# Score products of running streams on quarters of the TensorE columns, with the output projection and two norms laid between them

## The chip, the cores and the metric

The kernel runs on one core of one Trainium2 chip. The metric is the device time of one execution in microseconds (us). Five engines matter: TensorE (PE, with its weight load PEld), VectorE (DVE), ScalarE (ACT), GpSimd (POOL) and SyncE (SP), which here issues nearly all loads. Everything is in fp32: a matmul stands in the trace as two records, a transposition as one.

## The reference

One layer of a streaming encoder for 512 prompt rows and 8 running streams of 16 rows each (128 sample rows), so 640 rows of 1024 channels in 5 tiles of 128. The part around the change:

```python
q, k, v = parallel_mixer_inputs(...)           # 8 heads of 64, q and k normed
s = einsum('bqhd,bkhd->bhqk', q, concat(cache_k, k)) * 64**-0.5 + bias   # samples: 512 cached keys + 16 new
o = einsum('bhqk,bkhd->bqhd', softmax(s), concat(cache_v, v))
cat = concatenate([rms_norm(y_ssm, g1), rms_norm(y_att, g2)])            # 512 + 512 channels
x = x + cat @ w_out                                                      # 1024 x 1024
mk = rms_norm(mem_k, gain)                                               # memory keys, 256 tokens, 4 heads of 256
x = x + memory_attend(rms_norm(x), mk, mv)                               # cross-attention
x = x + hier_moe(rms_norm(x))
```

## The kernel before

The program is written out by hand for each engine. The function `pe_order` lists every product of TensorE up to the experts in the order in which it is made. Product number n goes to PSUM bank n mod 8; `claim(pe, key)` makes TensorE wait until the product eight places earlier in the list has been drained, and `done(eng, key)` makes another engine wait until a product is ready. So the list sets the order of the work and also who waits for whose bank. VectorE, ScalarE and GpSimd each run their own hand-written sequence, strictly in order.

The stages around the change are these.

- **Prompt attention.** 32 units (4 row tiles t by 8 heads). TensorE makes the scores of unit i (L926, key `S`), turns the probabilities of unit i-2 (L943, `PT`), and after every second unit makes their product with the values (L961, `PV`). VectorE adds the bias (L1873), takes the maximum (L1876, L1880) and the reciprocal of the sum (L1888); ScalarE does the exponential (L1313) and drains the turned tiles (L1330); GpSimd multiplies by the reciprocal (L1531). VectorE copies `PV` out (L1911).
- **Sample attention.** Eight steps, one for each stream b. `qblk` holds for each stream and each of the 4 head pairs a block 128 columns wide, zero outside the pair's own 32 columns; four matmuls add up into a 128 x 512 score tile `sA` (L971, the cached keys) and four into a 128 x 128 tile `sB` (L975, the new keys). The rest of the step works on earlier streams: turn the probabilities of b-1 (`sPa`, `sPb`, L943), multiply those of b-2 with the values (`sPV`, L989, 32 columns for each pair), transpose the result of b-3 (`sO`, L995), which VectorE copies out in `spv_out` (L1918). SP loads 1 MB of keys and 1 MB of values for each stream into two buffers each: keys b are issued once `sB` of b-2 is made, and values b once `sPV` of b-2 is made (L702, L707).
- Between the steps VectorE also does the **branch norms**: the squares of both 4 x 640 branch outputs, their sums over the 4 channel tiles (L1951), and the multiplication by the gains (L1956).
- **Output projection.** Ten pairs of products `oS` (state-space branch) and `oA` (attention branch), 4 matmuls of 128 x 512 each (L775). After the first four stands `ss` (L1020), ten matmuls of one column that finish the sums of squares. VectorE waits for GpSimd's inverse root (L1481) and adds every product to the residual rows (L2026, L2029). From the second row tile on, the finished rows are turned (`x1T`, L1001) and drained (L2000). Ahead of the third row tile VectorE norms the memory keys: squares and sums (L1599, L2008), then two multiplications for each of four parts (L1599, L2017). Then TensorE turns them (`mkT`, L1032).
- **The next stage** begins with the query projection `mq` of the cross-attention; its weights are loads 11 and 12 (L625). Load 11 waits for `ss`, load 12 for `oA` 8. After `mk_normed` GpSimd stores the memory keys and issues fourteen stores of zeros (L1537 to L1542).

The experts' stage at the end streams 96 MB of weights through five buffers.

```python
for a in range(NPAIR):   # sA of stream b, before
    last = nc.tensor.matmul(ps, qblk[:, b, a, :], kc[b % 2][:, a, :], start=(a == 0), stop=(a == 3))
```

Of the kernel before, what the change touches and what calls it, by code (L numbers as in the profile page):

```python
# [22 lines left out]
P = 128  # L23
D = 1024
# [54 lines left out]

def pe_order():  # L80
# [73 lines left out]
    for t in range(NT + 1):  # L154
# [6 lines left out]
        if t >= 1:  # L161
# [15 lines left out]
           11: ("ss", 0), 12: ("oA", 8), 13: ("oA", 9), 14: ("mq", 8)}  # L177
# [18 lines left out]
def program(nc, x_t, x_rows, mem_t, mem_rows, dense_w, exp_gu, exp_dn, ck_t, cv, cmk_t, cmv, cols, k_gain, mk_gain,  # L196
# [3 lines left out]
    with ctx:  # L200
# [131 lines left out]
        qblk = at(R + 10240, NB, NPAIR, P)  # L332
# [288 lines left out]
        def _(sp):  # L621
# [98 lines left out]
            sp.dma_start(mk_rows, mk_dram.ap().rearrange("(t p) d -> p t d", p=P)).then_inc(S["mem_landed"], 16)  # L720
# [50 lines left out]
        def _(pe):  # L771
# [193 lines left out]
            pe.wait_ge(S["qblk_ready"], 1)  # L965
            for b in range(NB + 3):
                if b < NB:
                    ps = claim(pe, ("sA", b))
                    pe.wait_ge(S[f"kc{b % 2}"], 16 * (b // 2 + 1))
                    for a in range(NPAIR):  # L970
                        last = nc.tensor.matmul(ps, qblk[:, b, a, :], kc[b % 2][:, a, :], start=(a == 0), stop=(a == 3))  # L971
                    last.then_inc(product_ready, 1)
                    ps = claim(pe, ("sB", b))
                    for a in range(NPAIR):
                        last = nc.tensor.matmul(ps[:, 0:P], qblk[:, b, a, :], kT[:, a, TP:T], start=(a == 0), stop=(a == 3))  # L975
                    last.then_inc(product_ready, 1)
# [28 lines left out]
            wo = [w_at(9), w_at(10)]  # L1005
            for t in range(NT + 1):
                if t < NT:

                    pe.wait_ge(S["branch_scaled"], 2 if t < NT - 1 else 3)
                    for c in range(2):  # L1010
                        for kind, k0, src in (("oS", 0, ysT), ("oA", 4, yaT)):
                            dense((kind, 2 * t + c), lambda k: src[:, k, tok(t)],
                                  lambda k: wo[c][:, k0 + k, :], 512, 4)
                if t == 0:

                    ps = claim(pe, ("ss", 0))
                    pe.wait_ge(S["sq_ready"], 3)
                    for br in range(2):
                        for j in range(NT):
                            last = nc.tensor.matmul(ps[:, br * NT + j:br * NT + j + 1], branch_sum[br][:, tok(j)], ones[:, 0:1],  # L1020
                                                    start=True, stop=True)
                    last.then_inc(product_ready, 1)
                if t >= 1:
                    for hh in range(2):
                        pe.wait_ge(drained["oA"], 2 * t - 1 + hh)
                        turn_rows("x1T", 2 * t - 2 + hh)
# [135 lines left out]
        def _(act):  # L1162
# [179 lines left out]
            for i in range(n + 2):  # L1342
                if 2 <= i < n:
                    exp_prompt(i)
                if i >= 2:
                    pt_out("PT", i - 2, i - 2, PROMPT_UNITS[i - 2][0] + 1)
            for b in range(NB + 2):
                if b < NB:
# [119 lines left out]
        def _(pool):  # L1468
# [120 lines left out]
        def _(dve):  # L1589
# [331 lines left out]
            attn_in(0)  # L1921
# [477 lines left out]
```

## Time and profile before

| | |
|---|---|
| three runs, median (lowest to highest) | 1109.52 us (1106.23 to 1111.93) |
| the profiled execution, its own time | 1107.45 us |
| its span, first to last instruction | 1105.7 us |
| PE, DVE, ACT, POOL busy | 88%, 38%, 18%, 15% |
| chain that ended last | PE 68%, DMA 16%, DVE 7% |
| mean granted clock of TensorE | 0.913 of full speed |

Times in the rows are microseconds from the start of the span. TensorE's granted clock is given as a share of 2.4 GHz, so 0.50 is 1.2 GHz. Busy shares are averages over stages; which wait ends last has to be read stage by stage.

### The profile page before, as it was taken

What the parts mean: (1) busy time and instruction counts of PE and PEld (TensorE: products, weight loads), DVE (VectorE), ACT (ScalarE), POOL (GpSimd) and SP (SyncE); (2) the same over time, 40 slices, a digit from 0 to 9 for tenths busy, and PEclk for the clock granted to TensorE, in tenths of its full rate; (3) what the DMA queues carried; (4) which work ended last, traced back from release to release, by engine and by line L of the source; (5) the groups of instructions that cost most, each with busy time, mean ns of one, the idle gap of its engine ahead of it and who ended that gap; (6) DMA issues with size and microseconds to landing.
All of it is one profiled execution on the core that took longest, in us unless ns stands there. A gap on an engine that the chain in (4) does not pass through costs nothing.

```text
span 1105.7 us, 12501 instructions
## 1 busy us (share of the span) xinstructions
PE 969.3 (88%) x4646; PEld 546.7 (49%) x4646; DVE 422.7 (38%) x1061; ACT 201.0 (18%) x450; POOL 165.7 (15%) x202
## 2 busy tenths in 40 slices
PE   6999988997989988899999898999389998797780
PEld 2444454544454455554544674455356565464350
DVE  1723638554254456335433531233633111110114
ACT  2311140214033312100100232011001111111110
POOL 0223100000034322204011330000101000000003
PEclk9999988998965589999999899999589999988895
DMA  9641324255330026725700436820559999999937
GB/s 358 258 55 60 79 91 157 95 175 202 153 152 1 1 77 232 301 78 205 289 0 18 174 143 238 371 85 20 220 207 425 426 425 425 424 425 427 427 162 285
DMA packets 45515, 230.67 MB, mean 209 GB/s; under 512 B 5632, under 2 KB 12296, under 8 KB 32960
## 3 DMA queue, kind: packets, MB, share of 16 engines
q1 hardware_dynamic: 33008, 185.94, 42.9%
q0 software_dynamic: 9712, 33.98, 9.1%
q10 hardware_dynamic: 2736, 9.96, 2.2%
q8 instruction: 38, 0.62, 0.2%
q14 instruction: 21, 0.17, 0.0%
HBM read 196.41 MB, written 31.35 MB: 206 GB/s over the span
## 4 chain that ended last, share of the span: by engine, by line
PE 68%; DMA 16%; DVE 7%; issue 3%; SPq 2%; POOL 2%; ACT 1%; POOLq 0%; DVEq 0%; ACTq 0%
PE banks L775 33%; DMA arena<-in_exp_gu 12%; PE banks L519 8%; PE banks L926 3%; PE banks L805 3%; PE banks L531 2%; PE banks L943 2%; DVE arena L1599 2%; SPq L676 2%; PE banks L961 2%; PE banks L971 1%; DMA arena<-in_ck_t 1%; PE banks L1081 1%; PE banks L1110 1%; DMA arena<-in_x_t 1%
## 5 line engine op out<-in xcount | busy, mean ns | idle before, releaser
L775 PE MATMUL banks<-arena 128*128 128x512 f32 (+1 forms) x976 | 416.8, 581 | 5.1 <-DVE arena L2043 3.0
L775 PEld LDWEIGHTS banks<-arena 128*128 128x128 f32 x976 | 182.4, 191 | 208.2 <-issue 203.5
L519 PE MATMUL banks<-arena 128*64 128x256 f32 (+1 forms) x1024 | 143.9, 400 | 25.0 <-DMA arena<-in_exp_gu 22.2
L519 PEld LDWEIGHTS banks<-arena 128*64 128x64 f32 (+1 forms) x1024 | 102.8, 155 | 72.7 <-issue 42.7
L1599 DVE TENSOR_TENSOR arena<-arena 128x16 f32<-128x16 f32 (+13 forms) x224 | 91.7, 410 | 87.7 <-ACT arena L1373 35.2
L531 PE MATMUL banks<-arena 128*64 128x512 f32 (+1 forms) x256 | 69.7, 600 | 9.0 <-ACT arena L1445 9.0
L2293 DVE SCALAR_TENSOR_TENSOR arena<-arena,banks 128x256 f32<-128x256 f32 x19 | 8.0, 421 | 162.4 <-ACT arena L1440 162.4
L1531 POOL TENSOR_SCALAR arena<-arena 128x128 f32<-128x128 f32 (+4 forms) x40 | 49.7, 1243 | 133.0 <-DVE arena L1888 133.0
L1567 POOL DMA_INDIRECT arena<-xn_scratch,tok_idx x19 | 18.6, 978 | 230.5 <-PE banks L513 209.6
L1480 POOL TENSOR_SCALAR arena<-arena 128x2 f32<-128x2 f32 (+4 forms) x30 | 6.3, 210 | 285.7 <-DVE arena L1792 114.7
L805 PE MATMUL banks<-arena 128*128 128x512 f32 x80 | 37.8, 635 | 9.5 <-DMA arena<-in_dense_w 8.5
L531 PEld LDWEIGHTS banks<-arena 128*64 128x64 f32 (+1 forms) x256 | 22.4, 146 | 44.4 <-issue 30.9
L1313 ACT ACTIVATE arena<-banks,arena 128x128 f32<-128x128 f32 (+3 forms) x48 | 25.1, 525 | 102.4 <-DVE arena L1880 96.5
L1876 DVE TENSOR_REDUCE arena<-banks 128x1 f32<-128x256 f32 (+3 forms) x68 | 32.0, 471 | 26.0 <-PE banks L1094 17.5
L943 PE MATMUL banks<-arena 128*128 128x128 f32 x120 | 30.1, 376 | 13.4 <-POOL arena L1531 13.3
L926 PE MATMUL banks<-arena 64*128 64x128 f32 (+3 forms) x64 | 41.8, 757 | 0.0
L943 PEld LDWEIGHTS banks<-arena 128*128 128x128 f32 x120 | 17.3, 181 | 40.1 <-issue 24.7
L1481 POOL TENSOR_TENSOR arena<-arena 128x2 f32<-128x2 f32 (+4 forms) x30 | 33.9, 1130 | 2.5
L1450 ACT ACTIVATE arena<-banks 128x512 f32<-128x512 f32 x38 | 22.7, 597 | 60.2 <-PE banks L531 60.2
L971 PE MATMUL banks<-arena 128*128 128x512 f32 x64 | 31.5, 636 | 1.8 <-DMA arena<-in_ck_t 1.8
L805 PEld LDWEIGHTS banks<-arena 128*128 128x128 f32 x80 | 16.1, 204 | 30.4 <-issue 28.6
L1873 DVE TENSOR_TENSOR banks<-banks,arena 128x128 f32<-128x128 f32 (+1 forms) x48 | 17.4, 362 | 29.9 <-PE banks L926 16.8
(277 smaller groups left out, 961.5 us busy)
## 6 DMA issues: line engine op xcount, KB each, us to landing
arena<-in_exp_gu SPq DMA_DIRECT2D x32, 2048.0 KB, 26.8
arena<-in_exp_dn SPq DMA_DIRECT2D x32, 1024.0 KB, 29.5
arena<-in_dense_w SPq DMA_DIRECT2D x14, 2048.0 KB, 9.8
moe_scratch<-arena ACTq DMA_DIRECT2D x19, 512.0 KB, 9.8
arena<-in_ck_t SPq DMA_DIRECT2D x8, 1024.0 KB, 7.2
arena<-in_cv SPq DMA_DIRECT2D x8, 1024.0 KB, 5.6
arena<-in_cmk_t SPq DMA_DIRECT2D x8, 1024.0 KB, 6.8
arena<-in_cmv SPq DMA_DIRECT2D x8, 1024.0 KB, 5.4
```

Source lines behind the costliest of these rows:

```text
L519: last = nc.tensor.matmul(banks[r0:r0 + n, 2 + half, 0:FF], x[:, k, r0:r0 + n], w[:, k, half * FF:(half + 1) * FF], start=(k == 0), stop=( ...
L531: last = nc.tensor.matmul(banks[r0:r0 + n, 6 + c, :], ht[:, f, r0:r0 + n], w[:, f, c * 512:(c + 1) * 512], start=(f == 0), stop=(f == 1))
L775: last = nc.tensor.matmul(ps[:, 0:n], lhs(i), rhs(i), start=(i == 0), stop=(i == k - 1))
L805: last = nc.tensor.matmul(ps, hT[:, k, tok(t)], w[:, k, :], start=(k == 0), stop=(k == KT - 1))
L926: nc.tensor.matmul(ps[:, 0:P * (t + 1)], qT[lo:lo + HD, h // 2, tok(t)], kT[lo:lo + HD, h // 2, 0:P * (t + 1)], start=True, stop=True).the ...
L943: last = nc.tensor.transpose(ps[:, a, :], Pb[unit % 3][:, (first + a) * P:(first + a + 1) * P], ident)
L971: last = nc.tensor.matmul(ps, qblk[:, b, a, :], kc[b % 2][:, a, :], start=(a == 0), stop=(a == 3))
L1313: ins = A(Pb[i % 3][:, c0:c0 + n], bank(key)[:, 0:n], ACT.Exp, bias=smax[:, i % 4, 2:3], accum_out=ssum[:, i % 4, j:j + 1])
L1481: g.tensor_tensor(dst, mean, minus_half[:, 0:n], ALU.pow).then_inc(signal, 1)
L1531: g.tensor_scalar(Pb[i % 3][:, 0:w], Pb[i % 3][:, 0:w], ssum[:, i % 4, 3:4], None, ALU.mult).then_inc(S["p_scaled"], 1)
L1599: link(v.tensor_tensor(o, a, b, op))
L1876: link(v.tensor_reduce(smax[:, i % 4, j:j + 1], ps[:, 0:n], AXX, ALU.max))
```

## The change

The score products of a sample write each head pair's 32 rows of the tile with a matmul of their own that uses a 32-column block of `qblk` (now 32 wide) and neither starts nor ends a sum with the others. The scores of stream 0 are made at the end of the prompt units. The output projection's products 0 to 7 of both branches, which read prompt rows alone, are listed in the sample steps (`OUT_FILL`): one `oS` and one `oA` in steps 1 to 8, `oS` 8 and 9 in steps 9 and 10. `ss` is split in two: nine columns ahead of step 1, one after the samples. The branch norms of the state-space half go to prompt units 4, 6 and 8, those of the attention half to units 12 to 14, 20 to 22, 28 to 30 and behind the last unit, and for the sample rows to the end. The sums for the memory keys are taken in VectorE's step 4, the multiplications in its steps 6 and 7, and their load moves up behind keys 2. Load 11 waits for the second `ss`.

```diff
 
+OUT_FILL = [[]] + [[("oS", i), ("oA", i)] for i in range(8)] + [[("oS", 8)], [("oS", 9)]]
...
     for i in range(10):
@@ -106,25 +109,24 @@
             o.append(("S", i))
         if 0 <= i - 2 < n:
             o.append(("PT", i - 2))
+        if i == n:
+            o += [("sA", 0), ("sB", 0)]
         if i >= 4 and (i - 4) % 2 == 1 and i - 4 < n:
             o.append(("PV", (i - 4) // 2))
+    o.append(("ss", 0))
     for b in range(NB + 3):
-        if b < NB:
+        if 0 < b < NB:
             o += [("sA", b), ("sB", b)]
+        o += OUT_FILL[b]
         if 0 <= b - 1 < NB:
             o += [("sPa", b - 1), ("sPb", b - 1)]
         if 0 <= b - 2 < NB:
             o.append(("sPV", b - 2))
         if 0 <= b - 3 < NB:
             o.append(("sO", b - 3))
-    for t in range(NT + 1):
-        if t < NT:
-            for c in range(2):
-                o += [("oS", 2 * t + c), ("oA", 2 * t + c)]
-        if t == 0:
-            o.append(("ss", 0))
-        if t >= 1:
-            o += [("x1T", 2 * t - 2), ("x1T", 2 * t - 1)]
+    o += [("x1T", i) for i in range(4)]
+    o += [("ss", 1), ("oA", 8), ("oA", 9)]
...
 W_AFTER = {3: ("u", 4), 5: None, 6: ("v", 4), 7: ("mk", 1), 8: ("mk", 3), 4: ("mv", 1), 9: ("mv", 3), 10: ("mv", 3),
-           11: ("ss", 0), 12: ("oA", 8), 13: ("oA", 9), 14: ("mq", 8)}
...
-        qblk = at(R + 10240, NB, NPAIR, P)
+        qblk = at(R + 10240, NB, NPAIR, 32)
+        key_sq = at(R + 11264, D)
...
             load_keys(2)
+            done(sp, ("PT", len(PROMPT_UNITS) - 1))
+            sp.dma_start(mk_rows, mk_dram.ap().rearrange("(t p) d -> p t d", p=P)).then_inc(S["mem_landed"], 16)
             for b in range(3, NB):
                 load_keys(b)
                 load_values(b - 1)
             load_values(NB - 1)
 
             done(sp, ("sB", NB - 1))
-            sp.dma_start(mk_rows, mk_dram.ap().rearrange("(t p) d -> p t d", p=P)).then_inc(S["mem_landed"], 16)
+            sp.wait_ge(S["mk_stats"], 1)
...
+            def sample_scores(b):
+
+                ps = claim(pe, ("sA", b))
+                pe.wait_ge(S[f"kc{b % 2}"], 16 * (b // 2 + 1))
+                for a in range(NPAIR):
+                    last = nc.tensor.matmul(ps[32 * a:32 * a + 32, :], qblk[:, b, a, :], kc[b % 2][:, a, :], start=True, stop=True)
+                last.then_inc(product_ready, 1)
+                ps = claim(pe, ("sB", b))
+                for a in range(NPAIR):
+                    last = nc.tensor.matmul(ps[32 * a:32 * a + 32, 0:P], qblk[:, b, a, :], kT[:, a, TP:T], start=True, stop=True)
+                last.then_inc(product_ready, 1)
+
+            def out_products(products):
+                for kind, i in products:
+                    wo = w_at(9 + i % 2, i < 2)
+                    k0, src, scaled = (0, ysT, 1) if kind == "oS" else (4, yaT, 5 if i < 8 else 6)
+                    pe.wait_ge(S["branch_scaled"], scaled)
+                    dense((kind, i), lambda k: src[:, k, tok(i // 2)], lambda k: wo[:, k0 + k, :], 512, 4)
+
+            def square_sums(i, columns):
+                ps = claim(pe, ("ss", i))
+                for br, j in columns:
+                    last = nc.tensor.matmul(ps[:, br * NT + j:br * NT + j + 1], branch_sum[br][:, tok(j)], ones[:, 0:1],
+                                            start=True, stop=True)
+                last.then_inc(product_ready, 1)
...
+                if i == n:
+                    pe.wait_ge(S["qblk_ready"], 1)
+                    sample_scores(0)
...
-            pe.wait_ge(S["qblk_ready"], 1)
+            pe.wait_ge(S["sq_ready"], 1 + NT - 1)
+            square_sums(0, [(0, j) for j in range(NT)] + [(1, j) for j in range(NT - 1)])
             for b in range(NB + 3):
-                if b < NB:
-                    ps = claim(pe, ("sA", b))
-                    pe.wait_ge(S[f"kc{b % 2}"], 16 * (b // 2 + 1))
...
+                if 0 < b < NB:
+                    sample_scores(b)
+                out_products(OUT_FILL[b])
                 if 0 <= b - 1 < NB:
...
-            wo = [w_at(9), w_at(10)]
-            for t in range(NT + 1):
-                if t < NT:
-
-                    pe.wait_ge(S["branch_scaled"], 2 if t < NT - 1 else 3)
-                    for c in range(2):
-                        for kind, k0, src in (("oS", 0, ysT), ("oA", 4, yaT)):
...
+            def x1_turn(i):
+                pe.wait_ge(drained["oA"], i + 1)
+                turn_rows("x1T", i)
+
+            for i in range(4):
+                x1_turn(i)
+            pe.wait_ge(S["sq_ready"], 1 + NT)
+            square_sums(1, [(1, NT - 1)])
+            out_products([("oA", 8), ("oA", 9)])
+            for i in range(4, 10):
+                x1_turn(i)
...
+                if i == n:
+                    exp_unit(n, [(("sA", 0), 512, 0), (("sB", 0), P, 512)])
...
-            pool.wait_ge(drained["ss"], 1)
-            rsqrt_mean(rstd_g, ssg, 2 * NT, AW, S["rstd_g_ready"])
-            pool.wait_ge(S["mk_stats"], 1)
-            rsqrt_mean(qf8, qss8, 8, MD, S["mk_factor"])
+                if i == n:
+                    pool.wait_ge(drained["ss"], 1)
+                    rsqrt_mean(rstd_g[:, 0:2 * NT - 1], ssg[:, 0:2 * NT - 1], 2 * NT - 1, AW, S["rstd_g_ready"])
+                if i == n + 4:
+                    pool.wait_ge(S["mk_stats"], 1)
+                    rsqrt_mean(qf8, qss8, 8, MD, S["mk_factor"], col=32)
+            pool.wait_ge(drained["ss"], 2)
+            rsqrt_mean(rstd_g[:, 2 * NT - 1:2 * NT], ssg[:, 2 * NT - 1:2 * NT], 1, AW, S["rstd_g_ready"], col=20)
             pool.wait_ge(S["mk_normed"], 4)
...
-                    c0 = (2 * a + h2) * SQ
-                    ins = v.tensor_copy(qblk[lo:lo + HD, :, a, c0:c0 + SQ],
+                    ins = v.tensor_copy(qblk[lo:lo + HD, :, a, SQ * h2:SQ * h2 + SQ],
...
+            def branch_step(i):
+
+                if i == 4:
+                    dve.wait_ge(drained["gv"], 4)
+                    dve.wait_ge(drained["gs"], 4)
+                    branch_squares(ysT, slice(0, T), 0)
+                if i == 6:
+                    branch_sums(0, slice(0, T))
+                if i == 8:
+                    branch_scale(ysT, out_ssm, slice(0, T))
+                t, step = (i - 12) // 8, (i - 12) % 8
+                cols = slice(t * P, (t + 1) * P)
+                if i >= 12 and step == 0:
+                    dve.wait_ge(drained["PV"], 4 * t + 4)
+                    branch_squares(yaT, cols, 1)
+                if i >= 12 and step == 1:
+                    branch_sums(1, cols)
+                if i >= 12 and step == 2:
+                    branch_scale(yaT, out_att, cols)
...
+                branch_step(i)
             attn_out(n - 1)
+            attn_in(n)
             pv_out(n // 2 - 2)
             pv_out(n // 2 - 1)
...
+            for i in (n + 4, n + 5, n + 6):
+                branch_step(i)
+
+            def out_rows(kind, i):
+                x = xr[:, i // 2, (i % 2) * 512:(i % 2 + 1) * 512]
+                col = i // 2 + (0 if kind == "oS" else NT)
+                done(dve, (kind, i))
+                if kind == "oA":
+                    dve.wait_ge(drained["oS"], i + 1)
+                v.scalar_tensor_tensor(x, bank((kind, i)), rstd_g[:, col:col + 1], x, ALU.mult, ALU.add).then_inc(drained[kind], 1)
...
+            def mem_key_sums():
+                dve.wait_ge(S["mem_landed"], 32)
+                for t in range(2):
+                    tt(key_sq, mk_rows[:, t, :], mk_rows[:, t, :], ALU.mult)
+                    ins = v.tensor_reduce(qss8[:, 4 * t:4 * t + 4], key_sq.rearrange("p (h d) -> p h d", h=MH), AXX, ALU.add)
+                    if t == 0:
+                        link(ins)
+                ins.then_inc(S["mk_stats"], 1)
+
+            def mem_key_rows(i):
+                seg = mk_rows[:, i // 2, (i % 2) * 512:(i % 2 + 1) * 512].rearrange("p (h d) -> p h d", h=2)
+                f = qf8[:, 4 * (i // 2) + 2 * (i % 2):4 * (i // 2) + 2 * (i % 2) + 2]
+                tt(seg, seg, spread(f.unsqueeze(2), [P, 2, MD]), ALU.mult)
+                v.tensor_tensor(seg, seg, spread(mkg.unsqueeze(1), [P, 2, MD]), ALU.mult).then_inc(S["mk_normed"], 1)
...
-            def norm_mem_keys():
-
-                dve.wait_ge(S["mem_landed"], 48)
...
-            for t in range(NT):
-                if t == 2:
-                    norm_mem_keys()
...
+            dve.wait_ge(S["x_landed"], 32)
+            for b in range(1, NB + 1):
+                attn_out(n + b - 1)
+                if b == 1:
+                    done(dve, ("ss", 0))
+                    ps = bank(("ss", 0))
+                    link(v.tensor_scalar(ssg[:, 0:NT], ps[:, 0:NT], 1.0 / 16, None, ALU.mult))
+                    v.tensor_copy(ssg[:, NT:2 * NT - 1], ps[:, NT:2 * NT - 1]).then_inc(drained["ss"], 1)
+                if b >= 2:
+                    dve.wait_ge(S["rstd_g_ready"], 1)
+                    out_rows("oS", b - 2)
+                    out_rows("oA", b - 2)
+                if b < NB:
+                    attn_in(n + b)
+                if b >= 3:
+                    spv_out(b - 3)
+                if b == 4:
+                    mem_key_sums()
+                if b >= 6 and b < 8:
+                    dve.wait_ge(S["mk_factor"], 1)
+                    mem_key_rows(2 * (b - 6))
+                    mem_key_rows(2 * (b - 6) + 1)
+            out_rows("oS", 7)
+            out_rows("oA", 7)
+            spv_out(NB - 2)
+            out_rows("oS", 8)
+            spv_out(NB - 1)
+
+            dve.wait_ge(drained["sO"], NB)
+            branch_squares(yaT, slice(TP, T), 1)
+            branch_sums(1, slice(TP, T))
+            branch_scale(yaT, out_att, slice(TP, T))
+            out_rows("oS", 9)
+            for i in range(4):
+                turn_out("x1T", i, norm_mem)
+            done(dve, ("ss", 1))
+            v.tensor_copy(ssg[:, 2 * NT - 1:2 * NT], bank(("ss", 1))[:, 2 * NT - 1:2 * NT]).then_inc(drained["ss"], 1)
+            dve.wait_ge(S["rstd_g_ready"], 2)
+            out_rows("oA", 8)
+            out_rows("oA", 9)
+            for i in range(4, 10):
+                turn_out("x1T", i, norm_mem)
```

## Rows read from the trace of the kernel before

**Rows 1.** Busy time of each engine by stage, with granted clock, DMA share and GB/s

```profile
318.00:338.00 20.00, 19.86 (x62) 9.31 (x63) 10.73 (x42) 7.12 (x27) 8.58 (x10) 0.50 0.25 95
395.00:464.00 69.00, 58.99 (x501) 36.79 (x498) 39.23 (x87) 16.13 (x56) 15.06 (x8) 0.91 0.59 211
464.00:541.00 77.00, 77.00 (x237) 38.55 (x236) 33.57 (x48) 7.09 (x13) 16.74 (x22) 1.00 0.55 204
```

**Rows 2.** Chain that ended last, samples to next stage: start, us, what

```profile
395.24 4.45 PE banks L971 x8
...
440.81 7.42 DMA arena<-in_ck_t
448.37 3.67 PE banks L971 x8
452.04 0.89 PE banks L975 x8
452.93 0.55 PE banks L943 x5
453.48 1.23 PE banks L989 x40
...
463.74 13.91 PE banks L775 x32
477.64 2.13 PE banks L1020 x20
...
537.44 1.75 PE banks L1001 x16
...
540.93 20.68 PE banks L775 x48
...
668.91 3.58 PE banks L1110 x16
```

**Rows 3.** VectorE's branch norms among the samples, by shape

```profile
L1951 DVE TENSOR_REDUCE arena<-arena 128x640 f32<-128x2560 f32 x1 | 4.6, 4564 | 0.0
...
L1599 DVE TENSOR_TENSOR arena<-arena 128x2560 f32<-128x2560 f32 x1 | 2.8, 2826 | 0.0
```

**Rows 4.** Timeline of the first prompt units, all engines

```profile
313.80 0.28 DVE L1873 TENSOR_TENSOR banks<-banks,arena 128x128 f32<-128x128 f32 x1
...
314.76 0.60 POOL L1531 TENSOR_SCALAR arena<-arena 128x128 f32<-128x128 f32 x1 [0.18 <-DVE arena L1888]
...
316.31 0.47 PE L943 MATMUL banks<-arena 128*128 128x128 f32 x1
...
324.03 0.69 PE L943 MATMUL banks<-arena 128*128 128x128 f32 x2
```

**Rows 5.** Timeline around the end of a sample step

```profile
437.23 0.80 PE L943 MATMUL banks<-arena 128*128 128x128 f32 x5 [2.12 <-POOL arena L1531]
...
437.96 2.36 PE L989 MATMUL banks<-arena 128*32 128x128 f32 x40
...
447.84 0.33 PE L995 MATMUL banks<-arena 128*128 128x128 f32 x1
...
448.21 0.46 DVE L1918 COPY arena<-banks 64x64 f32<-64x64 f32 x2 [1.64 <-PE banks L995]
...
448.89 0.16 DVE L1888 RECIPROCAL arena<-arena 128x1 f32<-128x1 f32 x1
```

**Rows 6.** VectorE's drain of one output product, by shape

```profile
L2026 DVE SCALAR_TENSOR_TENSOR arena<-banks,arena 128x512 f32<-128x512 f32 x10 | 7.5, 748 | 13.0 <-PE banks L775 10.6 <-POOL arena L1481 2.4
```

**Rows 7.** Timeline of VectorE at the memory keys

```profile
495.58 1.22 DVE L1599 TENSOR_TENSOR arena<-arena 128x1024 f32<-128x1024 f32 x1
...
499.35 1.22 DVE L2008 TENSOR_REDUCE arena<-arena 128x4 f32<-128x1024 f32 x1
502.61 0.69 DVE L1599 TENSOR_TENSOR arena<-arena 128x512 f32<-128x512 f32 x1 [2.04 <-POOL arena L1481]
```

**Rows 8.** Loads issued from 520 to 536 us: size, median us to landing

```profile
arena<-in_dense_w SPq DMA_DIRECT2D x1, 2048.0 KB, 9.5
```

More of the change, by code:

```diff
@@ L119, in pe_order @@
             o.append(("sO", b - 3))
-    for t in range(NT + 1):
-        if t < NT:
-            for c in range(2):
-                o += [("oS", 2 * t + c), ("oA", 2 * t + c)]
-        if t == 0:
-            o.append(("ss", 0))
-        if t >= 1:
-            o += [("x1T", 2 * t - 2), ("x1T", 2 * t - 1)]
+    o += [("x1T", i) for i in range(4)]
+    o += [("ss", 1), ("oA", 8), ("oA", 9)]
+    o += [("x1T", i) for i in range(4, 10)]
     o += [("mkT", i) for i in range(4)]
@@ L1002, in turn_rows @@
                 last.then_inc(product_ready, 1)
-            wo = [w_at(9), w_at(10)]
-            for t in range(NT + 1):
-                if t < NT:
-                    pe.wait_ge(S["branch_scaled"], 2 if t < NT - 1 else 3)
-                    for c in range(2):
-                        for kind, k0, src in (("oS", 0, ysT), ("oA", 4, yaT)):
[L1012 to L1026, printed above, removed]
+            def x1_turn(i):
[8 more added lines that the diff above has]
+                x1_turn(i)
             for i in range(4):
@@ L1347, in _ @@
             for b in range(NB + 2):
-                if b < NB:
+                if 0 < b < NB:
                     exp_unit(n + b, [(("sA", b), 512, 0), (("sB", b), P, 512)])
@@ L1919, in spv_out, with branch_squares, branch_sums, branch_scale @@
                 ins.then_inc(drained["sO"], 1)
+            link(v.tensor_scalar(out_ssm, out_ssm, 0.25, None, ALU.mult))
+            def branch_squares(y, cols, n_sums):
+                if n_sums:
+                    dve.wait_ge(S["sq_ready"], n_sums)
+                tt(branch_sq[:, :, cols], y[:, :, cols], y[:, :, cols], ALU.mult)
+            def branch_sums(br, cols):
+                v.tensor_reduce(branch_sum[br][:, cols], branch_sq[:, :, cols].rearrange("p k t -> p t k"), AXX, ALU.add
+                                ).then_inc(S["sq_ready"], 1)
+            def branch_scale(y, gain, cols):
+                w = cols.stop - cols.start
+                v.tensor_tensor(y[:, :, cols], y[:, :, cols], spread(gain.unsqueeze(2), [P, 4, w]), ALU.mult
+                                ).then_inc(S["branch_scaled"], 1)
+            def branch_step(i):
[16 more added lines that the diff above has]
+                    branch_scale(yaT, out_att, cols)
             attn_in(0)
@@ L1954, in branch_scale @@
-            def branch_scale(y, gain, cols):
-                w = cols.stop - cols.start
-                v.tensor_tensor(y[:, :, cols], y[:, :, cols], spread(gain.unsqueeze(2), [P, 4, w]), ALU.mult
-                                ).then_inc(S["branch_scaled"], 1)
-            for b in range(NB):
-                if b >= 1:
-                    attn_out(n + b - 1)
-                attn_in(n + b)
-                if b >= 3:
-                    spv_out(b - 3)
-                if b == 0:
-                    dve.wait_ge(drained["gv"], 4)
-                    dve.wait_ge(drained["gs"], 4)
-                    branch_squares(ysT, slice(0, T), 0)
-                if b == 1:
-                    branch_sums(0, slice(0, T))
-                if b == 2:
-                    branch_scale(ysT, out_ssm, slice(0, T))
-                if b == 3:
-                    dve.wait_ge(drained["PV"], len(PROMPT_UNITS) // 2)
-                    branch_squares(yaT, slice(0, TP), 1)
-                if b == 4:
-                    branch_sums(1, slice(0, TP))
-                if b == 5:
-                    branch_scale(yaT, out_att, slice(0, TP))
@@ L1981, in _ @@
-            attn_out(n + NB - 1)
-            for b in range(NB - 3, NB):
-                spv_out(b)
-            dve.wait_ge(drained["sO"], NB)
-            branch_squares(yaT, slice(TP, T), 2)
-            branch_sums(1, slice(TP, T))
-            branch_scale(yaT, out_att, slice(TP, T))
-            done(dve, ("ss", 0))
-            ps = bank(("ss", 0))
-            link(v.tensor_scalar(ssg[:, 0:NT], ps[:, 0:NT], 1.0 / 16, None, ALU.mult))
-            v.tensor_copy(ssg[:, NT:2 * NT], ps[:, NT:2 * NT]).then_inc(drained["ss"], 1)
@@ L2019, in _ @@
-            for t in range(NT):
-                if t == 2:
-                    norm_mem_keys()
-                for c in range(2):
-                    i = 2 * t + c
-                    x = xr[:, t, c * 512:(c + 1) * 512]
-                    done(dve, ("oS", i))
-                    v.scalar_tensor_tensor(x, bank(("oS", i)), rstd_g[:, t:t + 1], x, ALU.mult, ALU.add).then_inc(drained["oS"], 1)
-                    dve.wait_ge(drained["oS"], i + 1)
-                    done(dve, ("oA", i))
-                    v.scalar_tensor_tensor(x, bank(("oA", i)), rstd_g[:, NT + t:NT + t + 1], x, ALU.mult, ALU.add).then_inc(drained["oA"], 1)
-                if t >= 1:
-                    turn_out("x1T", 2 * t - 2, norm_mem)
-                    turn_out("x1T", 2 * t - 1, norm_mem)
@@ L2033, in _ @@
-            turn_out("x1T", 8, norm_mem)
-            turn_out("x1T", 9, norm_mem)
+            dve.wait_ge(S["x_landed"], 32)
[20 more added lines that the diff above has]
+                    mem_key_rows(2 * (b - 6) + 1)
```

30 lines of the change are left out of this document (1 added, 29 removed).

## The prediction

> **What bounds the kernel now.** I read the busy time by stage first. From 464 to 541 us, the output projection, TensorE is busy all of the time at full clock: only removed or overlapped work helps there. From 395 to 464, the samples, it is busy 59.0 of 69 us. In the early prompt units (318 to 338) it is busy all the time at a granted clock of 0.50, the 1.2 GHz level; VectorE is busy for 10.7 of those 20 us [rows 1]. Then the chain of waits. A sample step is 3.67 us of `sA`, 0.89 of `sB`, 0.55 of turns, 1.23 of `sPV`, and the chain also goes through a load of keys of 7.42 us; the chain leaves the samples at 463.74 and reaches `mq` at 540.93 with TensorE's work alone [rows 2]. So all that counts is when `mq` starts. What follows should move with it as a block, since its loads and table work hang on products of its own stage.
>
> **The scores.** `sA` is 4 matmuls of 512 columns, 3.67 us for 8 records; `sB` 0.89 [rows 2]. In quarters of 32 rows, the nearest rows are `sPV`, 40 records on four column quarters in 1.23 us, 31 ns each, and the half-array products of L1110, 16 records of 512 columns in 3.58 us, 224 ns each [rows 2]. One such record alone takes 13.91/32 = 435 ns [rows 2], so halves overlap twofold. I take 8 x 112 = 0.90 us for `sA` and 8 x 31 = 0.25 for `sB`: 1.15 instead of 4.56. The bounds: all serial, 4.56, and the ideal quarter, 4.56/4 = 1.14.
>
> **The steps.** An `oS`, `oA` pair costs 13.91/2 = 6.95 us [rows 2]. A full step is 1.15 + 6.95 + 0.55 + 1.23 + 0.3 (`sO`, [rows 5]) = 10.2 us; step 1 has no `sPV` and `sO` (8.7), step 2 no `sO` (9.9), steps 3 to 7 are full (51.0), step 8 has no scores (9.0), steps 9 and 10 have half a pair (5.0 and 3.8). Sum 87.4 us. The keys are now covered: keys b+1 are issued right behind values b-1, at the end of step b-1, so they have one step, 10.2 us, against the 7.42 of the row. The load of the memory keys, moved ahead of keys 3, adds 1 MB where steps 1 and 2 give it 18 us: nothing.
>
> **What is late instead: VectorE.** In each step VectorE ends with `spv_out`, which waits for `sO`, TensorE's last product of the step. Only then come the reciprocal for b and the drain of `oS` b-1. But `oS` b takes the very bank of `oS` b-1 from step 4 on (eight products a step, eight banks). The rows give, from the start of `sO` at 447.84, the reciprocal's end at 449.05 [rows 5]; 0.75 for the drain [rows 6] makes 1.96 us. TensorE wants the bank after 0.27 + 1.15, at 1.45. So steps 4 and 6 stall 0.5 us each. Behind `spv_out` of step 4 stand the sums for the memory keys, 495.58 to 500.57 = 4.99 us [rows 7]: step 5 stalls 5.5 us. Behind that of step 6 stand four multiplications of 0.69 [rows 7], 2.7 us: step 7 stalls 3.2. Step 8 has no scores, its banks are another eight, and it stalls nothing. Together 9.7 us. The cover for GpSimd's scaling and the exponential is the pair of products between them, 6.95 us: 1.9 and 1.4 us fit.
>
> **A rule weighed.** The rows show full 128-row products drained by one 0.75 us instruction each, and VectorE at 39 of 69 us [rows 1, 6]. By the Trainium skill, page TensorEngine Tiling (Array Packing), section PSUM Bottleneck, tiling speeds the matmuls but not the drain, and the drain may become the bound. By that rule the sum is the one above; without it these 9.7 us would be left out.
>
> **The clock.** After 2.12 us without work TensorE came back at half speed: five turns took 0.80 us and `sPV` 2.36, against 0.55 and 1.23 [rows 5, 2], about 1.7 us lost until it was back. I charge that three times: at the start of step 1, and after the stalls in steps 5 and 7. 5.1 us.
>
> **Prompt units.** Squares (2.83), sums (4.56) and gains (as long as the squares) of the 2560-wide branch enter units 4, 6, 8 [rows 3]: 10.2 us on VectorE. Unit 5's maximum, begun at 313.80 before, is held until 316.7; the probabilities of unit 4 then need 1.7 us (as from 313.80 to 314.76 + 0.60 and a hop), so their turn comes at 318.5 rather than 316.31 [rows 4]. Following the same order on through the sums and the gains, unit 8's turn comes at 330.4 instead of 324.03 [rows 4]: 6.4 us. The 512-wide pieces later cost 0.6 to 1.0 each and sit in the wait for an exponential, 0.3 us in all. Total 6.7; bounds 0 (all covered) and 10.2 (none).
>
> **The joint.** The last values' product ends at 395.24 + 6.7. `sA` and `sB` of stream 0 lie where TensorE waited for GpSimd; at half clock they last 2.3 us against a wait of 1.6: +0.7. Then TensorE waits for VectorE's copy, squares and sums of the last tile, 0.3 + 0.7 + 1.0 + hops = 2.2, and nine of `ss` take 2.0 [rows 2]. Step 1 starts at 406.8.
>
> **The tail.** 406.8 + 87.4 + 9.7 + 5.1 = 509.0 for the end of the last `sO`. Squares and sums of the sample rows are ready 2.4 us later; four `x1T` (0.44 each, 1.75 for four [rows 2]) hide most of that. The gain's multiplication lets `oA` 8 start at +3.1; `oA` 8 and 9 take 6.95, six `x1T` 2.6, `mkT` 1.75; the last drain on VectorE adds 0.3: 14.7. `mq` would start at 523.7. Load 11 is issued at about +3 and has 11.7 us; the row of a load in company of the zero stores says 9.5 [rows 8], but two 1 MB loads are just ahead and GpSimd's stores start at +8.5: I add 1 us, bounds 0 and 5. GpSimd's fourteen issues end about when the first `mq` is made, so its inverse root is in time. `mq` at 524.7 instead of 540.93: 16.2 us gained. The shorter clearing of `qblk` saves VectorE 2.6 us ahead of the gates, where TensorE's products end last: nothing.
>
> The profiled execution took 1107.45 us, so 1091.2; the median of the runs lies 2.1 higher, and I give **1093 us**.
>
> **Rivals.**
> - *The memory-key work is absorbed* (VectorE's drains come earlier than I read, or the banks fall otherwise): the 9.7 us of stalls and 3.4 of clock go away, 1080. For it: VectorE's own work per step is some 5 us of 10. Against: the order in the code, `sO` last.
> - *The quarters don't overlap with 512 columns.* Then scores cost 4.56 as before: 7 steps x 3.4 = 24 more, 2 at stream 0, but the stalls shrink by 7.6 and one clock dip goes: +16.5, 1109.5, no change. For it: no row has quarters with 512 columns. Against: halves with 512 do overlap [rows 2].
> - *Slower: the clock stays at half through steps 1 to 3* after the joint, where TensorE waits 2.2 us and then makes one-column products. Price: 28.6 us of work at double length, less the 1.7 counted: +27, 1120. It decides from 16 us of work at half beyond what I counted. For it: in the prompt units a busy TensorE stayed at 0.50 [rows 1]. Against: those are 64-row products; the dense ones of 464 to 541 ran at 1.00, and after the dip at 437 the clock was back within 3.5 us [rows 1, 2, 5].
> - *Smaller gain*: the prompt units lose all 10.2, and load 11 or 12 comes 5 us late: 1093 + 3.5 + 4 = 1100.
>
> **Chances.** A measurement here tells 0.5%, 5.5 us, from no change: faster is below 1104, slower above 1115. Forecast 0.58, absorbed 0.16, smaller gain 0.10, no overlap 0.09, half clock 0.07. So faster 0.83, same 0.10, slower 0.07. The range takes in the absorbed case less a little for a kinder prompt, 1078, and reaches just short of no overlap, 1106.
>
> **What would show it.** `sA` with 8 records in about 0.9 us; TensorE's idle in steps 5 and 7 of 5.5 and 3.2 us, released by VectorE's drain of `oS`, and half clock behind them; unit 8's turn at about 330; no key load in the chain; `mq` at 525. If `sA` takes 3.6 us, the first step of the sum is wrong; if step 5 shows no wait, the bank argument is; if the clock column reads 0.5 over several steps, the clock is the story.

## The result and the profile after

Over 20 runs of each kernel the changed one takes 1104.32 us (1102.24 to 1108.28) and the one before 1110.88 us (1105.89 to 1113.41). The ratio is 0.9952, with a 95% interval of 0.994 to 0.9965: about 5 us faster by the ratio and 6.6 by the medians, where the forecast had 16 of 1109. The time lies inside the range of 1078 to 1106, at its edge, because the range was wide; the forecast gain was two and a half to three times the measured one. The profiled execution has a span of 1102.4 us against 1105.7, only 3.3 less, so the ledger below adds up to 3.3.

The busy time by stage of the changed kernel, in the columns of [rows 1] (the stages are the same clock times, though the work in them has shifted):

```profile
318.00:338.00 20.00, 15.44 (x50) 7.48 (x48) 16.61 (x39) 5.45 (x23) 6.54 (x9) 0.50 0.25 91
395.00:464.00 69.00, 58.19 (x370) 30.29 (x371) 27.76 (x70) 12.38 (x40) 14.88 (x10) 0.88 0.37 138
464.00:541.00 77.00, 68.63 (x420) 36.26 (x419) 33.63 (x67) 14.47 (x36) 19.13 (x23) 0.93 0.58 222
```

In the prompt units VectorE's busy time has gone from 10.7 to 16.6 of 20 us and TensorE's has fallen from 19.9 to 15.4. From 464 to 541 us, where TensorE was busy all of the time before, it is now idle for 8.4 us; the granted clock of the two later stages is 0.88 and 0.93 where [rows 1] has 0.91 and 1.00.

The chain that ended last, from the joint to the cross-attention (start, us, what; it answers to [rows 2]):

```profile
404.30 4.00 PE banks L973 x18
408.30 1.86 PE banks L956 x8
410.16 0.43 PE banks L960 x8
410.59 8.75 PE banks L780 x16
...
431.02 7.07 PE banks L780 x16
...
451.60 1.24 DVE arena L1622
452.86 1.23 DVE arena L2016
454.11 1.24 DVE arena L1622
455.40 1.10 issue
...
456.88 0.76 DVE arena L2010
...
457.78 9.07 PE banks L780 x16
...
484.30 8.80 PE banks L780 x16
...
519.18 11.24 DMA arena<-in_dense_w
...
530.66 23.90 PE banks L780 x48
...
650.98 8.31 DMA arena<-in_cmk_t
659.43 5.48 PE banks L1111 x32
```

L973 is `ss`, L956 and L960 the quartered `sA` and `sB`, L780 the output products and `mq`. L1622 and L2016 at 451.60 to 456.5 are VectorE's squares and sums of the memory keys, and L2010 is its drain of an output product. A pair of output products takes 7.07 us at full clock; three of the eight take 8.75 to 9.07. No load of sample keys is among the waits on the way. At 519.18 the chain leaves TensorE for weight load 12, and `mq` starts at 530.66, where it started at 540.93 before.

TensorE's timeline in four places (start, us, what, in brackets the idle time ahead and what ended it) shows the joint, the stall in step 5, then the tail:

```profile
404.30 4.00 PE L973 MATMUL banks<-arena 128*128 128x1 f32 x18 [2.16 <-DVE arena L1952]
...
451.00 1.06 PE L956 MATMUL banks<-arena 128*32 128x512 f32 x8
...
457.78 2.90 PE L780 MATMUL banks<-arena 128*128 128x512 f32 x3 [5.50 <-DVE arena L2010]
...
514.85 0.38 PE L973 MATMUL banks<-arena 128*128 128x1 f32 x2 [0.60 <-DVE arena L1952]
515.45 7.13 PE L780 MATMUL banks<-arena 128*128 128x512 f32 x16 [0.21 <-DVE arena L1957]
...
525.04 1.91 PE L1049 MATMUL banks<-arena 128*128 128x128 f32 x16
530.66 23.90 PE L780 MATMUL banks<-arena 128*128 128x512 f32 x48 [3.71 <-DMA arena<-in_dense_w]
```

The quarters work: 8 records in 1.06 us instead of 3.67 [rows 2]. The wait of 5.50 us for VectorE's drain of `oS` (L2010) is the one forecast. The wait of 3.71 us for load 12, after `mkT` is done, is not.

### The profile page after: what moved, and what is told of

Read it like the earlier page. It is cut to its first block, busy times and chain, and to the rows that moved or that the text cites. A ratio compares the mean times of both kernels' runs of the same rounds, so it can differ in the third digit from the quotient of the medians.

```text
span 1102.4 us, 12542 instructions
## 1 busy us (share of the span) xinstructions
PE 949.5 (86%) x4646; PEld 531.5 (48%) x4646; DVE 420.1 (38%) x1071; ACT 201.8 (18%) x450; POOL 169.1 (15%) x204
## 4 chain that ended last, share of the span: by engine, by line
PE 67%; DMA 16%; DVE 8%; issue 4%; SPq 2%; POOL 2%; ACT 1%; POOLq 0%; DVEq 0%; ACTq 0%
PE banks L780 34%; DMA arena<-in_exp_gu 12%; PE banks L522 8%; PE banks L931 3%; PE banks L810 3%; PE banks L534 2%; DVE arena L1622 2%; PE banks L948 2%; SPq L679 2%; PE banks L1098 1%; PE banks L995 1%; PE banks L1127 1%; DMA arena<-in_x_t 1%; PE banks L1111 1%; PE banks L897 1%
## 5 line engine op out<-in xcount | busy, mean ns | idle before, releaser
L780 PE MATMUL banks<-arena 128*128 128x512 f32 (+1 forms) x976 | 426.8, 592 | 18.9 <-DVE arena L2010 9.9
L780 PEld LDWEIGHTS banks<-arena 128*128 128x128 f32 x976 | 185.4, 195 | 226.2 <-issue 221.4
L1622 DVE TENSOR_TENSOR arena<-arena 128x512 f32<-128x512 f32 (+12 forms) x227 | 92.2, 406 | 94.9 <-ACT arena L1392 41.8
L1550 POOL TENSOR_SCALAR arena<-arena 128x128 f32<-128x128 f32 (+4 forms) x40 | 52.2, 1305 | 167.6 <-DVE arena L1910 167.6
L2334 DVE SCALAR_TENSOR_TENSOR arena<-arena,banks 128x256 f32<-128x256 f32 x19 | 8.0, 421 | 162.5 <-ACT arena L1459 162.5
L810 PE MATMUL banks<-arena 128*128 128x512 f32 x80 | 36.2, 614 | 11.0 <-DMA arena<-in_dense_w 8.4
L1898 DVE TENSOR_REDUCE arena<-banks 128x1 f32<-128x256 f32 (+3 forms) x68 | 32.0, 471 | 29.3 <-PE banks L1111 20.7
L2337 DVE SCALAR_TENSOR_TENSOR arena<-arena,banks 128x256 f32<-128x256 f32 x19 | 8.0, 421 | 51.0 <-PE banks L522 51.0
L1347 ACT ACTIVATE arena<-banks 128x128 f32<-128x128 f32 (+3 forms) x48 | 19.7, 430 | 41.2 <-PE banks L948 41.2
## 6 DMA issues: line engine op xcount, KB each, us to landing
arena<-in_dense_w SPq DMA_DIRECT2D x14, 2048.0 KB, 10.2
```

The costliest lines, as they stand in the source:

```text
L780: last = nc.tensor.matmul(ps[:, 0:n], lhs(i), rhs(i), start=(i == 0), stop=(i == k - 1))
L810: last = nc.tensor.matmul(ps, hT[:, k, tok(t)], w[:, k, :], start=(k == 0), stop=(k == KT - 1))
L1550: g.tensor_scalar(Pb[i % 3][:, 0:w], Pb[i % 3][:, 0:w], ssum[:, i % 4, 3:4], None, ALU.mult).then_inc(S["p_scaled"], 1)
L1622: link(v.tensor_tensor(o, a, b, op))
L1898: link(v.tensor_reduce(smax[:, i % 4, j:j + 1], ps[:, 0:n], AXX, ALU.max))
```

## Experiments

All times are medians; the ratio is to the kernel before on the same chip. "The changed kernel" is 1104.3. A difference from it is taken between medians of different chips, on which the kernel before gave 1108.3 to 1110.9 us; by the ratios these differences come out up to 1.2 us otherwise.

**1. Key work ahead of the wait.** In VectorE's loop over the steps:

```diff
                 if b < NB:
                     attn_in(n + b)
-                if b >= 3:
-                    spv_out(b - 3)
                 if b == 4:
                     mem_key_sums()
...
                     mem_key_rows(2 * (b - 6))
                     mem_key_rows(2 * (b - 6) + 1)
+                if b >= 3:
+                    spv_out(b - 3)
```

> Memory-key sums and multiplications of VectorE put ahead of its wait for sO in steps 4, 6 and 7, where it is idle. Bank theory (TensorE's stalls in steps 5 and 7 come from work queued behind that wait): the gaps ahead of oS in steps 5 and 7 fall from 5.6 and 3.5 us to about 1, the half-clock pairs behind them (9.07 and 8.80 us) to 7.1; 11 us in all, 1093 against 1104. Rival (VectorE has no free 5 us in a step, the work only moves): the gaps stay or go to steps 4 and 6, no change.

Measured 1091.7 us, ratio 0.9832 (0.9804 to 0.986): 12.6 less than the changed kernel. TensorE's timeline at the same step:

```profile
451.75 1.07 PE L956 MATMUL banks<-arena 128*32 128x512 f32 x8
...
453.63 7.11 PE L780 MATMUL banks<-arena 128*128 128x512 f32 x16 [0.60 <-DVE arena L2010]
```

The gap falls from 5.50 to 0.60 us and the pair behind it from 9.07 to 7.11. The gap in step 7 falls from 3.25 to 0.60 us too, and those of steps 4 and 6 stay at 0.60. VectorE did have the time, ahead of its wait. The rival falls.

**2. Weight loads waited for singly.**

```diff
-            wq = [w_at(11), w_at(12)]
+            wq = [w_at(11), w_at(12, False)]
...
+                if i == 1:
+                    pe.wait_ge(w_landed[W_SLOT[12]], 16 * w_count(12))
```

> The first mq product waits for weight load 11 alone, the second for load 12. Theory of the double wait: mq starts at 527 instead of 530.7 without a pause, its first six products take 20.9 instead of 23.9 us, 6 to 7 us less in all. Rival (load 12 comes so late that the second product waits as long): it lands at 530.4 and the second product is due at 534, so this rival gives no gain only if the landing slips by over 3 us. Second rival: the gain is given back at the later wait for the sample memory keys.

Measured 1098.2 us, ratio 0.9892 (0.9863 to 0.992): 6.2 less. In its chain `mq` starts at once behind the last drain:

```profile
515.38 7.15 PE banks L780 x16
522.55 0.75 DVE arena L2012
523.30 3.60 DVE arena L2032 x6
526.95 20.87 PE banks L780 x48
```

3.7 us of waiting and 3.0 us of half clock behind it were the price, in the profiled executions, of one wait that stands one product too early. The load itself was in time for the product that needs it.

**3. `ss` behind the first product of step 1.**

```diff
-            pe.wait_ge(S["sq_ready"], 1 + NT - 1)
-            square_sums(0, ...)
...
+                if b == 1:
+                    out_products([("oS", 0)])
+                    pe.wait_ge(S["sq_ready"], 1 + NT - 1)
+                    square_sums(0, ...)
+                    out_products([("oA", 0)])
```

(and the same order in `pe_order`).

> The nine one-column products ss move behind sA, sB and oS of step 1. Theory (the wait for VectorE's sums at the joint empties TensorE, and the clock falls for ss and step 1): the wait of 2.1 us goes, ss takes 2 instead of 4.0 us, step 1's pair 7 instead of 8.75: 6 to 7 us less, about 1098. Rival (the clock is low there because of the prompt units before, whatever stands at the joint): only the 2.1 us go, ss and the pair stay at half clock.

Measured 1095.8 us, ratio 0.9865 (0.9835 to 0.9895): 8.5 less, a little over the 6 to 7. The timeline at the joint:

```profile
402.87 1.09 PE L994 MATMUL banks<-arena 128*64 128x128 f32 x16 [2.13 <-ACT arena L1350]
403.89 1.07 PE L955 MATMUL banks<-arena 128*32 128x512 f32 x8
404.77 0.40 PE L959 MATMUL banks<-arena 128*32 128x128 f32 x8
405.11 3.70 PE L779 MATMUL banks<-arena 128*128 128x512 f32 x8
408.64 2.06 PE L972 MATMUL banks<-arena 128*128 128x1 f32 x18
```

`sA` takes 1.07 us here and 1.86 in the changed kernel; `ss`, the same 18 records, 2.06 and 4.00. From the last values' product (L995, here L994) to the scores of step 2 the profiled execution of the changed kernel takes 18.8 us and this one 11.9, 6.9 less; what the medians have beyond that is not accounted for. The prompt units ahead are the same, and in the changed kernel the granted clock was 1.00 from 395 to 402.2 us, 0.86 on the mean of the second pause (402.2 to 404.3) and 0.50 from there on. So the clock fell in the 2.16 us of idle time at the joint, and the rival falls. A pause of 2.13 us just ahead of it, for ScalarE's drain of turned probabilities, stands in both runs and alone cost no clock here.

**4. The quarters alone**, in the kernel before: `qblk` 32 columns wide and the two score products written as in the change, nothing else.

> Kernel of before with nothing but the quartered score products. If the samples were bound by TensorE's work: 8 steps by 3.4 us, 27 us less than before, 1084. Bank-and-chain theory: TensorE already waited there for keys and for the chain through VectorE and GpSimd, which now bind; the keys' wait of 7.4 us and steps of about 7 us stay; 5 to 15 us less than before, with TensorE idle more and its clock at half in more of the stage.

Measured 1107.3 us against 1110.9, ratio 0.9982 (0.9958 to 1.0006): nothing that can be told from no change, less than either account had. Its busy time from 395 to 464 us:

```profile
395.00:464.00 69.00, 40.20 (x511) 23.71 (x508) 40.86 (x90) 16.70 (x56) 15.08 (x8) 0.78 0.59 215
```

TensorE's busy time falls from 59.0 to 40.2 us and its clock from 0.91 to 0.78, but the stage takes as long: it leaves the samples at 461.89 where [rows 2] has 463.74. Its chain shows what now holds it:

```profile
410.70 1.30 PE banks L943 x5
412.00 2.34 PE banks L989 x40
...
414.77 9.05 DMA arena<-in_ck_t
...
430.15 3.65 DVE arena L1950
...
434.16 1.90 POOL arena L1531
```

A key load of 9.05 us, the branch norm's long sums (L1950) and GpSimd's scaling, and turns and `sPV` at half clock (1.30 and 2.34 us for 0.55 and 1.23). What the matmuls give back, the chain through the others takes, all but 1.9 us in this profile.

**5. The branch norm in pieces.** Each 2560-wide instruction of the state-space branch becomes five of 512, one instruction a unit from unit 4 on, and the first two attention tiles move to units 19 and 23:

```diff
+                if 4 <= i < 4 + 3 * NT:
+                    j, step = (i - 4) // 3, (i - 4) % 3
+                    cols = slice(j * P, (j + 1) * P)
...
+                for t, first in enumerate((19, 23, 28, 36)):
```

> The three 2560-wide norm instructions of the state-space branch (in prompt units 4, 6, 8) become fifteen 512-wide ones, one a unit. Theory (an instruction of 2.8 to 4.6 us does not fit in a unit, one of 0.6 to 1.0 does): unit 8's turn at about 325 to 326 instead of 330.6, 4 to 6 us less, 1099. Rival (VectorE's total work in the early units is what counts, 10 us of it): the delay is the same but spread, no change.

Measured 1099.0 us, ratio 0.9901 (0.987 to 0.9932): 5.3 less. The turn of unit 8, first in the changed kernel's timeline:

```profile
330.60 0.66 PE L948 MATMUL banks<-arena 128*128 128x128 f32 x2 [0.94 <-POOL arena L1550]
```

and with the pieces:

```profile
325.36 0.69 PE L948 MATMUL banks<-arena 128*128 128x128 f32 x2
```

Unit 8's turn comes at 325.36, 1.3 us behind the 324.03 of before [rows 4] instead of 6.6. From 318 to 338 us VectorE is busy no less than in the changed kernel (17.18 against 16.61 us), yet TensorE is busy for 18.59 us instead of 15.44. This speaks for the length of the single instruction and against the sum. It is not a clean separation: by unit 8 only five of the fifteen pieces have been made, and two tiles of the attention half have moved as well. And of the 5.2 us at unit 8 only 2.3 reach the joint: the last values' product ends at 399.81 instead of 402.14. From 331 to 392 us TensorE is busy all of the time in both runs, at a mean granted clock of 0.52 in the changed kernel and 0.50 here.

**6. Whole-column scores in the changed kernel.** `qblk` 128 wide again, four products adding up; the squares of the memory keys go to another buffer, since `qblk` takes the place of theirs.

> The changed kernel with score products over all 128 columns, as before. Theory (with output products between, TensorE's work is the bound of the steps): scores 3.4 us longer in seven steps, 24 us, less what the stalls of steps 4 to 7 absorb (7 to 8 us) and a clock dip: 13 to 18 us more than the changed kernel, 1119. Rival (the quarters give nothing, as when they stand alone): no change against the changed kernel.

Measured 1118.1 us, ratio 1.0082 (1.0049 to 1.0115): 13.8 more than the changed kernel. In its profiled execution `mq` starts at 544.30 instead of 530.66, 13.6 us later. The quarters, worth nothing that can be told alone, are worth 14 us once output products stand between the steps. The changed order without them is slower than the kernel before.

**7. The first, second, third and fifth together.**

> Key work ahead of the wait, weight loads waited for singly, ss behind the first product, norm in pieces, all in one. If the four losses lie one behind another on the one chain, the gains add: 12.6 + 6.2 + 8.5 + 5 = 32 us less than the changed kernel, 1072. If they share a cause (one clock dip counted twice, or a DMA that binds next), less: 1080 or more.

Measured 1076.3 us, ratio 0.9703 (0.9678 to 0.9729): 28.0 less, of 32.6 that the four add up to (by the ratios 27.6 of 35.3). It lies between the 1072 of gains that add and the 1080 of gains that share a cause, and decides for neither. In this profile, whose execution took 1080.4 us and was the slowest of the five, `mq` starts at 508.16 without a pause. The first output product of step 1 took 4.58 us where experiment 3 shows 3.63: in this execution part of the clock's loss at the joint was still there. The missing 4.6 us are not accounted for.

**8. And the drains ahead of the sample copy.**

```diff
                     out_rows("oA", b - 2)
+                if b >= 4:
+                    spv_out(b - 4)
                 if b < NB:
                     attn_in(n + b)
...
-                if b >= 3:
-                    spv_out(b - 3)
```

> As the four together, and VectorE drains the output products before it waits for the sample result, which is copied one step later. Bank theory: the remaining gaps of 1.3 to 1.7 us ahead of oS in steps 4 to 7 go, 4 to 6 us less than the four together, 1067. Rival: the gaps have another cause (the scores' own bank or the key loads) and stay.

Measured 1072.2 us, ratio 0.9676 (0.9647 to 0.9705): 4.2 less than the four together, and the fastest version here, 3.2% below the kernel before. Its chain in step 4 is TensorE's work alone:

```profile
441.07 0.99 PE banks L955 x8
442.07 0.22 PE banks L959 x8
442.29 7.06 PE banks L779 x16
449.35 0.55 PE banks L947 x5
...
451.38 1.00 PE banks L955 x8
```

One step lasts 10.31 us (441.07 to 451.38). With the four together it lasted 10.95, 0.60 of it the wait for the drain of `oS`. So steps 4 to 7 account for 2.6 of the 4.2 us, and the expected gaps of 1.3 to 1.7 us were smaller. The profiles differ by another 1.7 us in step 1, where this execution shows no clock dip behind the same pause; nothing in the edit explains that.

**9. The zero stores later.** GpSimd's clearing of a tile and its fourteen stores go behind the ten query norms.

> The changed kernel with GpSimd's clearing of the zero tile and its fourteen stores moved behind the ten query norms, out of the time in which load 12 lands. If those stores slow load 12: it lands in 8 to 9.5 us instead of 11.2, mq waits about 1 to 2 us instead of 3.7 and may stay at full clock, 2 to 6 us less. If its own predecessor (load 11 and the 1 MB loads ahead) slows it: it stays at 11 us and nothing changes.

Measured 1109.1 us, ratio 1.0003 (0.9988 to 1.0018): 4.7 more than the changed kernel. Load 12 took as long as before, and the stores found a worse place:

```profile
520.12 11.18 DMA arena<-in_dense_w
...
608.93 10.05 POOL moe_scratch L1570 x14
```

The zero stores are not what makes load 12 long. What does stays open: load 11 is still landing for the first 4 us of it, and GpSimd's 1 MB store of the memory keys is issued beside it in both runs; neither was moved. The zero stores' issue takes GpSimd 10.05 us, and there the first scaling of the cross-attention waits behind it.

**10. The changed kernel again.**

> The changed kernel once more on this chip, for its own scatter: 0.995 of before; mq again waits for load 12 behind a landing of 10.5 to 11.5 us, and the sample memory keys of the cross-attention land in 7.2 to 8.3 us with the products behind them at half clock (5.4 us instead of 3.67). If the last is chance, it is absent here.

Measured 1104.1 us, ratio 0.996 (0.9937 to 0.9982). `mq` again waits for load 12, landing after 11.44 us. The cross-attention differs:

```profile
651.64 7.09 DMA arena<-in_cmk_t
...
658.87 3.67 PE banks L1111 x32
...
674.36 8.31 DMA arena<-in_cmv
```

The keys land in 7.09 us instead of 8.31 and the products behind them run at full clock, but a value load is waited for instead. From the end of the first six `mq` products to the next dense stage (690.09 in the changed kernel, 693.70 before) it was 132.1 us before, 135.5 in the changed kernel and 133.7 here; experiment 4, whose code from the output projection on is that of before, shows 133.6. In experiments 1 to 3 and 5 to 8 it was 133.8 to 136.8. So part of what was lost there is scatter of the loads' landing and of the clock, but no run of the changed order reaches the 132.1.

## Why the prediction was wrong

**Right: which stage, the quarters, the steps.** 1.15 us was forecast for `sA` and `sB`; the chains at full clock have 0.99 + 0.22. Pairs take 7.06 instead of 6.95. Experiment 6 gives the quarters' worth in this order, 13.8 us; the rival of serial quarters, put at 16.5, is out.

**Right: VectorE is late next.** The stall in step 5, forecast at 5.5 us, is 5.50; the one in step 7, forecast at 3.2, is 3.25; the small ones, forecast at 0.5, are 0.6. Experiment 1 removes the large ones and their clock dips, leaves a small stall in each of the four steps and gains 12.6 us; the forecast's 9.7 and 3.4 less four small stalls of 0.5 make 11.1, and from step 1's scores to the last `sO` its profiled execution is 11.2 us shorter. What the medians have beyond that is not accounted for. The Trainium skill, page TensorEngine Tiling (Array Packing), section PSUM Bottleneck, says that tiling speeds up TensorE but not PSUM evacuation, and that the copy may become the bottleneck. This trace agrees in part: the 5.50 us end with a drain. But the drain instruction, 0.76 us, was as long as before (0.75 in [rows 6]), and it emptied a full-width product; it came late because it stood behind the memory-key work in VectorE's queue.

**Right: the prompt units.** Unit 8's turn was forecast at 330.4 and came at 330.6; the end of the last values' product, forecast at 401.9, came at 402.14. Experiment 5 bears the mechanism out at unit 8 and leaves open how much of the loss reaches the joint.

**Mis-sized: "I charge that three times", 5.1 us for the clock.** Measured against the full-clock figures of the forecast: `ss` 4.00 instead of 2.0, step 1's scores 2.29 instead of 1.15 and its pair 8.75 instead of 6.95, the pairs of steps 5 and 7 9.07 and 8.80 instead of 6.95. Together 8.9 us, 3.8 more than charged. What was overlooked is that the wait at the joint comes ahead of `ss`, so `ss` itself, the scores and the first part of the pair ran at 1.2 GHz (granted clock 0.50 from 404.3 until about 414 us, 1.00 from there on): one dip cost 4.9 us there, not 1.7. With a few tenths the other way, the last `sO` ended at 512.5 instead of 509.0.

**Wrong: "Load 11 ... has 11.7 us", the step on the weights.** The sum priced load 11 alone and gave load 12 no term (only the rival "smaller gain" names it), though the code waits for both ahead of the first `mq`. Load 11 itself was in time: it was issued at 515.27 and took 8.2 us, and `mkT` ended at 526.95. Load 12 is issued when `oA` 8 is made. Before, 10.3 us of work lay between that and `mq` (530.6 to 540.93) and the load's 9.5 us [rows 8] just fitted. The change took `oS` 9 out of that stretch, leaving 7.8 us from 519.18 to the end of `mkT` at 526.95, and the load took 11.2. So TensorE waited 3.7 us and then ran six products in 23.9 instead of 20.7 us: 6.9 us against the 1 charged. Experiment 2 shows it, with 6.2 us.

**Not foreseen: 3.4 us in the cross-attention.** "What follows should move with it as a block" failed by this much, a term that the sum put at nothing. The stage waits for sample memory keys in both kernels, 3.56 us before and 5.05 now, and after the longer wait 32 records took 5.48 instead of 3.67 us. Experiments 4 and 10 show that 1.5 to 1.8 us of such a difference come by themselves: in experiment 4, with the code of before, 3.62 us of waiting were followed by 5.36 us for the 32 records. Whether the rest follows from the change stays open.

The ledger of the profiled executions: 16.2 forecast, less 3.5 at the last `sO`, plus 0.2 in the tail, less 2.7 and 3.2 at load 12 (the wait beyond the 1 charged, and the clock), less 3.4 in the cross-attention, less 0.3 in the experts' stage: 3.3 us.

The rival "smaller gain", 1100, came nearest, and in one of its two halves: a load was late, by 3.7 us, but the prompt units lost 6.9 us and not all 10.2. The lower rival, "the memory-key work is absorbed", did not happen, but experiment 1 shows that most of it needs only another place in VectorE's order. The half clock through whole steps did not come; pairs of dense products were back at 7.06 us one step later.

## What to carry to other kernels

When work is moved out of a stretch, look at what was hidden behind that stretch: a load issued at its start and awaited at its end loses its cover, and a wait for two loads ahead of the first use is a wait for the later one. On an engine that runs in order, put work that is free to move ahead of the wait for the latest product, not behind it, and cut it to the size of the gaps. Idle time of 2 us or more on TensorE can bring a clock dip behind it, as some of such pauses here did and others did not; it is to be priced with everything that runs in that dip.

## What the runs showed of the hardware

Quartered fp32 products of 512 columns overlap nearly four at a time: 8 records in 0.99 us, where one full-width record takes 0.43 and eight quarters of that would be 0.87. TensorE's clock after a wait: in the changed kernel 2.16 us of idle time were followed by 4.00 us of one-column products, 2.29 of scores and a slow pair, at a granted clock of 0.50 until about 414 us. The pause ahead of the last values' product was 2.59 us in experiment 7 and 2.60 in experiment 8; `sA` of step 1, right behind that product, took 1.56 us in the one and 1.07 in the other. In the cross-attention 3.56 us of waiting (before) and 3.83 (experiment 10) were followed by 3.67 us for 32 records, 3.62 (experiment 4) by 5.36 and 5.05 (the changed kernel) by 5.48. So the length of the wait alone does not tell. The two waits in the cross-attention, from the timeline of before:

```profile
664.87 3.67 PE L1094 MATMUL banks<-arena 128*64 128x256 f32 x32 [3.56 <-DMA arena<-in_cmk_t]
```

and of the changed kernel:

```profile
659.43 5.48 PE L1111 MATMUL banks<-arena 128*64 128x256 f32 x32 [5.05 <-DMA arena<-in_cmk_t]
```

Two 2 MB loads issued 3.9 us apart landed in 8.2 and 11.2 us; the second took 11.18 us when the zero stores beside it had been moved away, with the 1 MB store of the memory keys still there.
